# Queries' root taken into the exponentials' scale, and turned rows, low halves and output products placed anew, in a two-block fp32 kernel

## What is computed

```python
def first_block(x, ...):                    # 2 layers
    q, k, v, qi, ki, wi, u, vs = split(x @ w_in)
    a = dsa_attention(rope(q), rope(k), v, rope(qi), rope(ki), wi)
    b = spatial_gating(gelu(u), gelu(vs), ...)
    x = layer_norm(ALPHA * x + concat(a, b) @ w_o)
    ...                                     # gated MLP, per-layer embedding, layer_norm

def second_block(x, c, ...):                # layer 0 even, layer 1 odd
    for layer in range(2):
        h = modulate(rms_norm(x, norm_mix), sh1, sc1)
        y = even_mixer(h) if layer == 0 else odd_mixer(h)
        x = x + g1 * y
        h = modulate(rms_norm(x, norm_mlp), sh2, sc2)
        x = x + g2 * (relu(h @ w1) ** 2 @ w2)

def rms_norm(x, w):
    return x * rsqrt(mean(x * x) + 1e-6) * w

def even_mixer(h):                          # MLA, 8 heads of 64 + 32, and a dilated mixture
    q = (rms_norm(c_q) @ w_uq)              # 8 heads of 96
    k, v = (rms_norm(c_kv) @ w_ukv), k_r    # 64 of keys and 64 of values a head; 32 shared
    q, k = rms_norm(q, mla_qn), rms_norm(k, mla_kn)
    q, k = rope on the last 32 of each head
    o_a = softmax(q k^T / sqrt(96), causal) v
    o_b = dilated_mixture(rope(rms_norm(qd)), rope(rms_norm(kd)), vd)   # 3 groups x 4 heads
    return concat(o_a, o_b) @ w_out

def odd_mixer(h):                           # difference of two maps, and block attention
    qc, kc = rope(rms_norm(qc)), rope(rms_norm(kc))        # 4 heads x 2 maps of 64
    p = softmax(qc kc^T / 8, causal)
    o_c = (p[map 0] - lam * p[map 1]) vc
    o_c = rms_norm(o_c, diff_subln) * (1 - lam_init)
    o_d = causal attention(rope(rms_norm(qm)), rope(rms_norm(km)), vm)  # 8 heads of 64
    return concat(o_c, o_d) @ w_out
```

## Time and profile before

| | |
|---|---|
| median of 3 runs | 1349.02 us (1345.61 to 1351.86) |
| the profiled execution | 1350.45 us, its span 1348.6 us |
| mean granted clock of TensorE | 0.987 |
| busy: TensorE / VectorE / ScalarE / GpSimd | 1291.3 / 922.1 / 653.7 / 114.0 us |
| chain that ended last, by engine | TensorE 79%, VectorE 12%, ScalarE 5% |

### The profile page before, as it was taken

The page is one execution under the profiler, slowest core; times in us unless marked ns, Lnnn a source line. Parts: engine busy times, 40 slices in busy tenths (PEclk is TensorE's granted clock), DMA queues, the critical chain, the costliest instruction groups (busy, mean ns, idle before and its releaser), DMA issues.

```text
span 1348.6 us, 15871 instructions
## 1 busy us (share of the span) xinstructions
PE 1291.3 (96%) x6342; PEld 1065.4 (79%) x6342; DVE 922.1 (68%) x1237; ACT 653.7 (48%) x884; POOL 114.0 (8%) x146
## 2 busy tenths in 40 slices
PE   8999999998999999999999899999999968999998
PEld 6878888887877888887788777888878756888886
DVE  6968777766787677775778747766667874744444
ACT  6645444442563544444564536545446553654542
POOL 2001000001001000000334100000004400000000
PEclk9999999999999999999999989999999988999999
DMA  9626677864634678884353205867755411444450
GB/s 377 236 75 227 240 304 302 319 247 156 213 115 147 207 295 307 310 307 162 112 189 125 79 32 189 323 268 272 289 218 187 157 63 34 183 171 183 180 187 32
DMA packets 41113, 270.35 MB, mean 200 GB/s; under 512 B 4656, under 2 KB 4672, under 8 KB 12880
## 3 DMA queue, kind: packets, MB, share of 16 engines
q1 hardware_dynamic: 38288, 259.83, 52.2%
q0 software_dynamic: 2464, 8.98, 1.8%
q10 hardware_dynamic: 288, 0.52, 0.1%
HBM read 268.27 MB, written 1.05 MB: 200 GB/s over the span
## 4 chain that ended last, share of the span: by engine, by line
PE 79%; DVE 12%; ACT 5%; issue 2%; POOL 1%; DMA 0%; ACTq 0%; DVEq 0%; POOLq 0%
PE ps L1573 47%; PE ps L1563 24%; PE ps L1587 4%; DVE WB L1888 3%; PE ps L1675 2%; ACT E L1688 1%; PE ps L1650 1%; ACT WB L1688 1%; DVE st L2104 1%; POOL st L1490 1%; ACT H L1688 1%; DVE st L2174 1%; DVE SCR L2006 1%; ACT XTH L1688 1%; DVE H L2258 0%
## 5 line engine op out<-in xcount | busy, mean ns | idle before, releaser
L1888 DVE TENSOR_TENSOR WB<-RAW,WB 128x2048 fp32r<-128x2048 f32 (+3 forms) x211 | 452.8, 2151 | 235.9 <-ACT WB L1688 235.6
L1688 ACT ACTIVATE WB<-RAW 128x2048 fp32r<-128x2048 f32 (+3 forms) x211 | 379.9, 1802 | 218.5 <-PE ps L1573 214.8
L1563 PE MATMUL ps<-WB,XTH 128*128 128x512 f32 (+3 forms) x1176 | 314.0, 388 | 9.3 <-ACT XTH L1688 4.4
L1573 PE MATMUL ps<-WB,XTH 128*128 128x512 f32 (+3 forms) x1176 | 306.6, 382 | 9.7 <-DVE WB L1888 9.6
L1573 PE MATMUL ps<-WB,XTL 128*128 128x512 f32 (+3 forms) x1176 | 304.4, 380 | 0.9 <-DVE XTL L1961 0.5
L1573 PEld LDWEIGHTS ps<-WB,XTH 128*128 128x128 f32 x1176 | 218.1, 189 | 53.8 <-DVE WB L1888 15.2
L1563 PEld LDWEIGHTS ps<-WB,XTH 128*128 128x128 f32 x1176 | 213.6, 190 | 49.5 <-ACT XTH L1688 7.8
L1573 PEld LDWEIGHTS ps<-WB,XTL 128*128 128x128 f32 x1176 | 219.0, 189 | 40.3 <-DVE XTL L1995 0.8
L1563 PE MATMUL ps<-WB,HTH 128*128 128x512 f32 (+1 forms) x452 | 126.9, 396 | 0.6 <-ACT HTH L1688 0.5
L1573 PE MATMUL ps<-WB,HTH 128*128 128x512 f32 (+1 forms) x452 | 126.5, 395 | 0.0
L1573 PE MATMUL ps<-WB,HTL 128*128 128x512 f32 (+1 forms) x452 | 126.4, 394 | 0.0
(11 more groups left out here) (179 smaller groups left out, 961.3 us busy)
## 6 DMA issues: line engine op xcount, KB each, us to landing
RAW<-W SPq DMA_DIRECT2D x220, 1024.0 KB, 4.9
RAW<-W SPq DMA_DIRECT2D x22, 768.0 KB, 4.3
VEC<-vecd POOLq DMA_DIRECT2D x10, 512.0 KB, 6.5
RAW<-W SPq DMA_DIRECT2D x8, 512.0 KB, 3.7
RAW<-W SPq DMA_DIRECT2D x4, 576.0 KB, 3.7
RAW<-W SPq DMA_DIRECT2D x2, 648.0 KB, 3.9
T<-sgwd POOLq DMA_DIRECT2D x2, 512.0 KB, 8.5
...
```

Source lines behind the costliest of these rows:

```text
L1563: eng.matmul(banks[b][:, 0:cw], x2[j][0], hi[:, j, c0:c0 + cw], start=first and j == 0, stop=False)
L1573: op = eng.matmul(banks[b][:, 0:cw], x2[j][0 if low_w else 1], (lo if low_w else hi)[:, j, c0:c0 + cw], start=False, stop=last and end and ...
L1688: return eng.activation(dst, src, f, **k)
L1888: eng.tensor_tensor(WB[:, it["raw"], 0:w], RAW[:, it["raw"], 0:w], WB[:, it["high"], 0:w].bitcast(F32), ALU.subtract).then_inc(*up("wl", n))
```

## The change

It has three parts.

*Arithmetic of the roots.* The queries of MLA, of the difference and of the block attention are no longer multiplied by their root. The root stays a column per head (`RQ`); the exponentials take it as their scale, read from that column (constants such as 96 ** -0.5 or 0.125 are in it), and the negated maxima are multiplied by it, in one operation with two tensors (`scalar_tensor_tensor`). For MLA the product of both norms' weights for the 64 unrotated columns goes into the keys' norm, made once by GpSimd (`both_norms`, 128x64), so that VectorE multiplies only 8 x 32 elements of the queries by a weight, and the rotation waits for the sum and not for the root.

*Arithmetic of the difference.* The exponentials of the first map stay as they are: the second map's are multiplied by lambda times the ratio of the two sums, in one operation with the addition. The sums of the first map drop out in the norm that follows, if its eps is multiplied by their square, which two small operations of VectorE do (`diff_out`); GpSimd's first operation goes there (`root`).

*Order.* `linear_k` takes a written list of steps in place of `ready` and `out_start`. `quiet` is gone, and `soon` has come: in a step k in `soon` the oldest pending low half is issued right behind the scores. The tables change in both layers. Turned queries of the second tile move ahead of the first scores. In the even layer the turned groups of tile 0 move from `ahead[6]` to `between[5]`. In the odd layer 24 large products of the fill move from k = 2 to later steps, and the norm behind the difference is placed at `between[5]` and `between[7]`. One pair of padding products goes in the even layer and two in the odd one, and ScalarE copies all high halves of turned rows of the second block's output projection. In the first block one turn stands ahead of values, and a high half of weights ahead of a copy.

The core of the diff:

```diff
-        def linear_k(name, lhs, evac, ready, turned=False, by_tile=True):
-            its = chunk_items(name)
+        def linear_k(name, lhs, evac, turn_rows, steps):
+            its = {it["a"]: it for it in chunk_items(name)}
...
+            for a, t, *mm_ in steps:
+                if not mm_:
+                    turn_rows(a, t)
+                    yield
+                    continue
...
             cur["lag"] = True
             for k in range(n + 2):
-                cur["quiet"] = k in quiet
                 for f in ahead.get(k, ()):
                     f()
                 if k < n:
                     scores(units[k], 0 if k else first)
                 old = list(low)
+                if k in soon:
+                    lows(old[:1])
                 for f in between.get(k, ()):
                     f()
...
                 if k in flush:
-                    lows(old)
+                    lows([it for it in old if it in low])
...
-                do("rsqrt", ("qk", key), r, 1.0 / hd, 1e-6, ("qk_sum", key))
+                do("rsqrt", ("qk", key), r, *((1.0 / hd, 1e-6) if roots is None else (1.0, hd * 1e-6)), ("qk_sum", key))
...
-                do("qk_rope", key, x, nh, hd, hf, r0, cos, sin, w, r, list(scr["free"]))
+                do("qk_rope", key, x, nh, hd, hf, r0, cos, sin, w, None if roots is not None else r, list(scr["free"]))
...
-                ahead = {6: [lambda: turn_groups(0)]}
-                between = {0: [lambda: turn_heads(1)], 6: [lambda: turn_groups(1)]}
-                steps = (4, 3, 2, 2, 2, 1, 1, 0, 2, 1, 1, 1, 1, 1, 1, 1)
-                pads, flush, quiet = (), (0, 1, 2, 3, 6, 7, 8, 9, 10, 11), (4,)
+                ahead = {0: [lambda: turn_heads(1, 0)]}
+                between = {0: [lambda: turn_heads(1, 1)], 5: [lambda: turn_groups(0)], 6: [lambda: turn_groups(1)]}
+                steps = (4, 3, 2, 2, 2, 1, 0, 1, 1, 1, 0, 0, 1, 1, 0, 0)
+                flush, soon = (0, 1, 2), (5, 6, 7, 8, 9, 10, 11)
...
-                ahead = {}
-                between = {0: [lambda: turn_qk(tw, 1, (0, 0), (1, 4)), ch[3, 0][0], ch[3, 1][0]],
+                ahead = {0: [lambda: turn_qk(tw, 1, (0, 0))]}
+                between = {0: [lambda: turn_qk(tw, 1, (1, 4)), ch[3, 0][0], ch[3, 1][0]],
                            1: [ch[3, 0][1], ch[3, 1][1], ch[4, 0][0], ch[4, 1][0]],
                            2: [ch[4, 0][1], ch[4, 1][1], lambda: turn_qk(tw2, 0, (3, 8)), lambda: turn_qk(tw2, 1, (3, 8))],
-                           3: [lambda: turn_qk(tw2, 0, (4, 12)), lambda: turn_qk(tw2, 1, (4, 12))]}
-                steps = (1, 1, 1, 1, 1, 1, 2, 1, 1, 1, 1, 1)
-                pads, flush, quiet = (0, 0, 0, 2), (0, 1, 5, 6, 7), (3,)
+                           3: [lambda: turn_qk(tw2, 0, (4, 12)), lambda: turn_qk(tw2, 1, (4, 12))],
+                           5: [lambda: normed.pop(0)()], 7: [lambda: normed.pop(0)()]}
+                steps = (1, 1, 0, 1, 1, 0, 1, 1, 1, 1, 1, 0)
+                flush, soon = (0, 1), (4, 6, 7, 8, 9)
...
+            out_ = proj((0, 0), (0, 0, 0), (0, 1), (4, 0), (4, 0, 0), (0, 1, 0), (4, 1), (4, 1, 0))
...
+            def both_norms():
+                on.wait_ge(*at("small", 0))
+                qn, kn = sm["mla_q_norm_2"][:, 0:64], sm["mla_k_norm_2"][:, 0:64]
+                eng.tensor_tensor(kn, kn, qn, ALU.mult).then_inc(*up("both_norms", 0))
...
+                        if u["roots"] is None:
+                            scale = u["scale"]
+                        else:
+                            n2 = u["roots"][0].shape[2]
+                            scale = u["roots"][0][:, k // n2, k % n2:k % n2 + 1]
+                        op = act(E[:, i, o:o + nk], banks[b][:, c:c + nk], ACT.Exp, bias=bias, scale=scale,
                                  accum_out=total)
...
-                eng.reciprocal(r4, u["s4"]).then_inc(*own.up())
+                eng.reciprocal(r4, u["s4"][:, 2:4]).then_inc(*own.up())
                 on.wait_ge(*own.at())
                 on.wait_ge(*at("lam", 0))
-                eng.tensor_scalar(c2, r4[:, 2:4], lam[:, 1:2], None, ALU.mult).then_inc(*own.up())
-                on.wait_ge(*own.at())
-                for n_ in range(2):
-                    e1 = E[:, i, (2 + n_) * nk:(3 + n_) * nk]
-                    eng.tensor_scalar(e1, e1, c2[:, n_:n_ + 1], None, ALU.mult).then_inc(*own.up())
+                eng.scalar_tensor_tensor(out=c2, in0=u["s4"][:, 0:2], scalar=lam[:, 1:2], in1=r4, op0=ALU.mult, op1=ALU.mult
+                                         ).then_inc(*own.up())
...
-                on.wait_ge(*at("rsqrt", ("qk", key)))
-                eng.tensor_tensor(x3, x3, r.unsqueeze(2).broadcast_to([128, nh, hd]), ALU.mult).then_inc(*own.up())
-                on.wait_ge(*own.at())
+                if r is None:
+                    on.wait_ge(*at("qk_sum", key))
+                else:
+                    on.wait_ge(*at("rsqrt", ("qk", key)))
+                    eng.tensor_tensor(x3, x3, r.unsqueeze(2).broadcast_to([128, nh, hd]), ALU.mult).then_inc(*own.up())
+                    on.wait_ge(*own.at())
```

159 lines of the change are left out of this document (92 added, 67 removed).

## The result

The changed kernel ran in **1331.62 us** (median of 4 runs, 1331.24 to 1332.32), the kernel before beside it in 1347.89 (4 runs, 1345.61 to 1351.86): a ratio of 0.9877 with a 95% interval of 0.9852 to 0.9902, some 16 us. The profiled execution took 1331.24 us, its span 1329.4, against 1350.45 and 1348.6.

A forecast was written before the change was run, and what follows sets the result against it. TensorE bounds the kernel (1291.3 of 1348.6 us busy); its idle time and slow clock can be won. 2.0 - 0.4 + 3.3 + 2.2 = 7.1, plus 0.5 for low halves, is 7.6 off the median 1349.02: 1341.4, range 1331 to 1348.5.

The forecast's parts named there:

- the 0.54: Chance given to a faster kernel: 0.16 for the clock that holds plus 0.38 beyond 6.7 us.
- forecast case: Whole kernel: the summed terms win 7.6 us, to 1341.4, likeliest 1336 to 1345; chance 0.54.
- the clock holds: Rival, both attentions: 4.9 and 5.2 us of clock loss also go, 17.7 us in all, 1331; chance 0.16.
- Heads: Even layer's latents and heads, 692 to 717: less VectorE work per query tile wins 2.0 us, bounds 0.6 and 2.9.
- it can come forward by 0.57 only: Head stage, first tile: VectorE's sum at 699.07 must await ScalarE's square of the keys, begun at 697.66, taking 0.84 us.
- Pointer scale: Exponentials of MLA and the odd layer: 93 ns more each, 4.5 us on ScalarE, charged -0.4 us, between 0 and -1.5.
- Even attention: 756 to 809: waits 6.0 instead of 7.0, one padding pair, one slow stretch gone; 3.3 us won, bounds 0 and 8.2.
- the long one to stay: Even attention: of two slow stretches the long one remains, between products at about 770 and 789; its loss is 4.9 us.
- Odd attention: 1072 to 1145: -0.5 for waits, 1.2 for padding, 1.5 for clock; 2.2 us won, bounds -6 and 8.
- The waits move, and their sum hardly changes: Odd attention: a new 7.1 us wait replaces those for the norm; waits total 17.9 us against 17.4.
- Only exchanged: Rival: heads yield their lower bound, slow stretches number as before, otherwise only pads' 2.4 us are won; 1346.6, chance 0.21.
- falls for longer: Rival, both attentions: half speed lasts longer, 11.2 us more loss against 4.4 won elsewhere; +6.8, 1355.8; chance 0.09.

## Why the prediction was right, and where it failed

The measured 1331.62 lies at the fast end of the range (1331.0 to 1348.5), on the side of the 0.54. The forecast gain was 7.6 us, the measured one 16. The forecast case by itself (1336 to 1345) missed. That the time is the 1331 of the rival "the clock holds" is luck in good part: only the even half of that rival came, and 6.9 us of less idle time in the heads and the odd stage, where I had 1.5, made up the rest. By the prediction's own signs the sum is wrong: the one wait of 7 us is two of 3.73 and 2.09, and no slow stretch is left in the even attention. Three signs came: no wait for the norm above 1 us in the odd attention, 17 us at half speed in both attentions together, and exponentials at about 0.45 us. The idle time of the heads fell further than to 2 us, to 1.04 in a stretch of 36.80.

- **Heads**: 2.0 us. The three waits of the earlier trace rows (1.97, 0.59, 0.92) are now 1.00, none and none, 2.5 us; the stretch is 3.3 shorter. Right in kind and too small. What failed is "it can come forward by 0.57 only": the square at 697.66 is not the one that VectorE sums at 699.07. That is the queries' square, done at 696.40, and in the changed kernel VectorE sums it before the keys' square has begun:

```profile
695.55 0.85 ACT L1688 ACTIVATE E<-H 128x768 f32<-128x768 f32 x1
...
703.12 1.75 DVE L1888 TENSOR_TENSOR WB<-RAW,WB 128x1536 fp32r<-128x1536 f32 x1
```

```profile
694.18 0.85 ACT L1715 ACTIVATE E<-H 128x768 f32<-128x768 f32 x1
...
696.17 0.94 DVE L2291 TENSOR_REDUCE st<-E 128x8 f32<-128x768 f32 x1
...
696.29 0.84 ACT L1715 ACTIVATE E<-GB 128x768 f32<-128x768 f32 x1
...
700.21 1.75 DVE L1922 TENSOR_TENSOR WB<-RAW,WB 128x1536 fp32r<-128x1536 f32 x1
```

  Counted from the start of this stretch (687.58 and 686.22) the low half behind the first tile comes 1.55 us earlier, all of what VectorE saves on one tile, against the 1.47 of the prediction. The 0.5 for the waits for low halves behind it did not come: in the changed kernel they are 1.08 and 0.75, before 1.08 and 0.60, and a wait of 0.63 for an exponential is new.
- **Pointer scale**: the 128-wide exponentials of the second block take 424 ns in the mean against 365:

```profile
L1715 ACT ACTIVATE E<-ps,st 128x128 f32<-128x128 f32 x36 | 14.9, 424 | 20.1 <-DVE st L2154 14.4 <-DVE st L2149 5.7
```

  12 of these 36 have a constant scale, so the other 24 cost (424 - 365) x 36 / 24 = 89 ns more each; I had taken 93. (The Trainium skill, ScalarE: Activation LUTs, What ACT_TABLE_LOAD costs, puts each pointer operand at about 93 ns; the trace agrees.)
- **Even attention**: I gave it 3.3 us, the stretch gained 8.6. The step that failed is "the long one to stay". I expected 4.9 us of clock loss there "between the products at about 770 and those at 789", and reasoned from which operations stand there. What the runs showed to matter is how long TensorE is idle between them: the waits in that place are 0.98 us now where they were 1.83 and 1.64, and padding in those two places alone kept the clock up in the profiled execution. The waits themselves I had at 6.0; they are 5.1 (45.50 us less 40.36 busy in 751 to 796.5).
- **Odd attention**: 2.2 us forecast, 6.0 gained. "The waits move, and their sum hardly changes" was wrong: idle time fell by 4.2 us. The hole was where I said, ended by what I said, and large products at 1.2 GHz followed; but it measured 3.73 + 2.09 instead of 7.1, because the first tile's keys can be turned while the second tile's are rotated, and I had let both wait for the end of the chain. The later waits for exponentials and copies were 0.70, 1.97, 1.15, 1.76 and 2.10, 7.7 in all, where I had walked to 10.8. The clock returned nothing (16.7 us at half speed before, 17.0 now), where I had 1.5: three slow stretches, not two.
- **First block**: 0 forecast. In the three profiles with its old order it ends at 687.58, 687.71 and 687.73, in the eleven with the new one between 685.86 and 687.15. The two profiles of the changed kernel alone differ by 0.9 (686.22 and 687.11), and only the later has the 3.4 us at half speed near 336 us that the kernel before has too. Like with like the new order is some 0.4 to 0.8 us earlier; the rest of the 1.4 goes with that slow stretch.
- **Rivals**: "the clock holds" came true in the even layer alone. TensorE's work there is 6.6 us less; without 0.6 of padding and the 1.7 already in the forecast that leaves 4.3 of the 4.9 I had put on it. "Only exchanged" and "falls for longer" did not occur: in the odd layer the loss stayed the same. The stretch 765.7:784.1 has 40 turns among its 139 matmul records (8 of them of the gain), 5.4 of its 17.0 busy us, and keeps the clock. (The Trainium skill, TensorE: Matmul & The Clock Gate, Part 4: PE-mode transpose, says that transposes don't count as busy in the same way; with so many other matmuls between them, no run here shows it or speaks against it.)

For the even layer the runs show that filling two pieces of idle time between short operations keeps the clock up, and that each of two moves of the table costs 3 to 5 us when it is put back. What stays open is which of the two waits matters more in the kernel before, since both were padded at once; what part the earlier large products have by themselves, since the padding products are wide too and the run with late products also waits longer; and where that run's three slower executions lost their time. What one slow stretch in the first block (3.4 us long, at about 10 or 336 us in several of the profiles) hangs on was not tried.
